# Attention stage: which engine copies the turned probabilities, in which order, and what is loaded first

## The reference, cut to what matters

```
q, k = rms_norm(q, q_gain), rms_norm(k, k_gain)      # per head, 64 channels
q, k = rotate own tokens by their angles (cos, sin)  # x*cos + quarter_turn(x)*sin
for each block of 128 queries:
    own block:     keys = own tokens at distance <= 128, and all context tokens
    context block: keys = all context tokens
    s = q @ k.T * 64**-0.5        (masked outside the window)
    p = softmax over keys and one extra "sink" logit per head (the sink's share is dropped)
    o = p @ v
```

## Time and profile before

| | us |
|---|---|
| median of 3 runs (5364.80 to 5377.84) | 5374.77 |
| the profiled execution | 5348.35 |
| its span in the trace | 5346.5 |
| attention stage, 3246.3 to 3589.7 from the span's start | 343 |

### The profile page before, as it was taken

The page is one execution under the profiler, slowest core; times in us unless marked ns, Lnnn a source line. Parts: engine busy times, 40 slices in busy tenths (PEclk is TensorE's granted clock), DMA queues, the critical chain, the costliest instruction groups (busy, mean ns, idle before and its releaser), DMA issues. The chain is left out here.

```text
span 5346.5 us, 88289 instructions
## 1 busy us (share of the span) xinstructions
PE 4436.9 (83%) x38298; PEld 3427.1 (64%) x38298; DVE 2537.0 (47%) x3635; ACT 1577.8 (30%) x2467; POOL 509.3 (10%) x483
## 2 busy tenths in 40 slices
PE   5999968888887687865878866768999899687999
PEld 4888757777776455652222344447888788576787
DVE  4556666667664674532000033554444322476553
ACT  3222223333322453421000032433222212563322
POOL 0000011100110465000000001330000000000000
PEclk8999979999998799987999977889999999898999
DMA  6656710000001110423999531112112133212232
GB/s 227 236 197 218 265 46 14 14 14 14 14 6 36 36 50 30 173 92 120 422 422 422 232 124 52 33 52 73 64 64 69 62 110 127 76 46 84 85 102 92
DMA packets 169889, 616.55 MB, mean 115 GB/s; under 512 B 24176, under 2 KB 37489, under 8 KB 144177
## 3 DMA queue, kind: packets, MB, share of 16 engines
q1 hardware_dynamic: 156224, 551.37, 28.4%
q0 software_dynamic: 13296, 59.77, 2.8%
HBM read 533.32 MB, written 77.75 MB: 114 GB/s over the span
## 5 line engine op out<-in xcount | busy, mean ns | idle before, releaser
L1885 PE MATMUL f_acc<-f_a_lo,f_w_hi 128*128 128x512 f32 x4048 | 1027.3, 356 | 65.6 <-DVE f_a_lo L2107 31.6
L1885 PEld LDWEIGHTS f_acc<-f_a_lo,f_w_hi 128*128 128x128 f32 x4048 | 666.4, 190 | 189.4 <-issue 43.5
L1885 PE MATMUL f_acc<-f_a_lo,f_w_lo 128*128 128x512 f32 x2288 | 687.9, 356 | 0.0
L1874 DVE TENSOR_TENSOR f_w_lo<-f_w_raw,f_w_hi 128x1024 fp32r<-128x1024 f32 (+1 forms) x176 | 228.4, 1298 | 527.5 <-ACT f_w_hi L1869 527.5
L1885 PEld LDWEIGHTS f_acc<-f_a_lo,f_w_lo 128*128 128x128 f32 x2288 | 377.1, 189 | 62.4
L1869 ACT CAST f_w_hi<-f_w_raw 128x1024 fp32r<-128x1024 f32 (+1 forms) x176 | 194.5, 1105 | 593.5 <-DMA f_w_raw<-in_ffn_w_up 209.9
L1885 PE MATMUL i_acc<-i_x_hi,i_w_hi 128*128 128x512 f32 (+1 forms) x1024 | 306.1, 354 | 12.2 <-DVE i_x_lo L2640 11.9
L335 DVE COPY_PREDICATED rw_work<-rw_mask_x,rw_big 128x512 f32<-128x512 uint8 x288 | 238.7, 881 | 154.5 <-PE rw_big L626 149.3
L1885 PE MATMUL i_acc<-i_x_lo,i_w_hi 128*128 128x512 f32 (+1 forms) x1024 | 304.9, 353 | 0.0
L1885 PE MATMUL i_acc<-i_x_hi,i_w_lo 128*128 128x512 f32 (+1 forms) x1024 | 304.7, 353 | 0.0
L1389 PE MATMUL ex_big<-ex_w,ex_xe_now 128*64 128x512 f32 x1024 | 237.6, 619 | 76.5 <-DMA ex_w<-in_exp_w 76.5
(11 more groups left out here) (521 smaller groups left out, 8036.4 us busy)
## 6 DMA issues: line engine op xcount, KB each, us to landing
ex_w<-in_exp_w SPq DMA_DIRECT2D x192, 1024.0 KB, 17.5
i_mod_rows<-in_ada_rows SPq DMA_DIRECT2D x128, 512.0 KB, 4.9
f_w_raw<-in_ffn_w_up SPq DMA_DIRECT2D x88, 512.0 KB, 3.3
i_w_raw<-in_w_in_both SPq DMA_DIRECT2D x44, 512.0 KB, 3.7
f_w_raw<-in_ffn_w_down SPq DMA_DIRECT2D x32, 704.0 KB, 4.1
i_w_raw<-in_w_in_lat SPq DMA_DIRECT2D x40, 512.0 KB, 4.8
pt<-i_stage POOLq DMA_DIRECT2D x22, 768.0 KB, 6.3
f_w_raw<-in_hgrn_w_both SPq DMA_DIRECT2D x24, 512.0 KB, 3.2
```

The costliest lines, as they stand in the source:

```text
L1874: dve.tensor_tensor(self.view(self.w_lo, u), self.view(self.w_raw, u), self.view(self.w_hi, u).bitcast(F32), ALU.subtract).then_inc(self.r ...
L1885: op = pe.matmul(acc[:, a:b], part[:, k], xs[:, k0 + k, a:b], start=(first and k == 0 and part is w_hi and xs is x_hi), stop=(last and k = ...
```

## The change

It makes three edits, all in `attention`.

1. The second group of turned tiles (k = 1), which the pairs with 512 and 640 columns have, is copied by ACT and not by DVE. The copy stands first in ACT's step, ahead of `exponentials(s+2)` or `logs(s+2)`. It has a semaphore of its own, so PE waits for two semaphores where it waited for one; `copies_until` counts both. 32 of 48 pairs have such a copy.
2. On DVE `copy_turned(s, 0)` stands ahead of `denominators(s+1)`.
3. `load(0)` is issued ahead of the constants. These are on two semaphores: four that the sums need (`first_in`) and four others (`const_in`). PE starts its loop after `first_in`; ACT starts after the small memset of DVE; the scores and the cosines wait for `consts_done` themselves.

```diff
+        def copies_until(n, k):
+            act_share = sum(1 for m in range(n) if len(turns(m % BLOCKS)) > 1) + (k > 1)
+            return turned_until[n] + k - act_share, act_share
...
-                for dst, src in ((ident, "ident"), (blockones, "blockones"), (turn, "turn"), (cos, "cos"), (sin, "sin"), (mask, "window")):
-                    sp.dma_start(dst[:], consts[src]).then_inc(S["const_in"], 16)
-                sp.dma_start(sink[:], sinks).then_inc(S["const_in"], 16)
-                sp.dma_start(gain[:], gains).then_inc(S["const_in"], 16)
...
                 load(0)
+                for dst, src in ((blockones[:], consts["blockones"]), (ident[:], consts["ident"]), (gain[:], gains), (turn[:], consts["turn"])):
+                    sp.dma_start(dst, src).then_inc(S["first_in"], 16)
+                for dst, src in ((cos[:], consts["cos"]), (sin[:], consts["sin"]), (mask[:], consts["window"]), (sink[:], sinks)):
+                    sp.dma_start(dst, src).then_inc(S["const_in"], 16)
                 load(1)
...
                 def consts_prepared():
-                    dve.memset(eps[:], 1e-6)
-                    dve.wait_ge(S["const_in"], 128)
+                    dve.wait_ge(S["first_in"], 64)
+                    dve.wait_ge(S["const_in"], 64)
...
                 def copy_turned(s, k):
+                    if k == 1:
+                        return
...
+                dve.memset(eps[:], 1e-6).then_inc(S["eps_done"], 1)
                 consts_prepared()
                 for s in STEPS:
                     groups = len(turns(pair_of(s)[1])) if kind(s) == "pair" else 0
+                    if groups:
+                        copy_turned(s, 0)
                     if kind(s + 1) == "pair":
                         denominators(s + 1)
-                    if groups:
-                        copy_turned(s, 0)
...
+                def copy_turned(s):                      # on ACT
+                    n = index(s)
+                    tiles = turns(pair_of(s)[1])[1]
+                    act.wait_ge(S["pt_ready"], turned_until[n] + 2)
+                    act.copy(pt_s[:, n % 2, tiles[0] * CH:(tiles[-1] + 1) * CH], big[:, T_BANK, 0:len(tiles) * CH]).then_inc(S["pt_copied_act"], 1)
...
-                act.wait_ge(S["consts_done"], 1)
+                act.wait_ge(S["eps_done"], 1)
                 square(0)
                 for s in STEPS:
+                    if kind(s) == "pair" and len(turns(pair_of(s)[1])) > 1:
+                        copy_turned(s)
                     if kind(s + 2) == "pair":
                         exponentials(s + 2)
...
                 def cosines(g):                          # on POOL
                     pool.wait_ge(S["normed"], g + 1)
+                    pool.wait_ge(S["consts_done"], 1)
...
                     pe.wait_ge(S["roped"], g + 1)        # in scores
+                    pe.wait_ge(S["consts_done"], 1)
...
                     if turned_until[n] + k:              # in turned
-                        pe.wait_ge(S["pt_copied"], turned_until[n] + k)
+                        by_dve, by_act = copies_until(n, k)
+                        pe.wait_ge(S["pt_copied"], by_dve)
+                        if by_act:
+                            pe.wait_ge(S["pt_copied_act"], by_act)
...
                     if first:                            # in values
-                        pe.wait_ge(S["pt_copied"], turned_until[n + 1])
+                        by_dve, by_act = copies_until(n + 1, 0)
+                        pe.wait_ge(S["pt_copied"], by_dve)
+                        pe.wait_ge(S["pt_copied_act"], by_act)
...
-                pe.wait_ge(S["consts_done"], 1)
+                pe.wait_ge(S["first_in"], 64)
```

More of the change, by code:

```diff
@@ L1498, in attention @@
         S = {n: ctx.sem(f"at_{n}") for n in (
-            "const_in head_in0 head_in1 consts_done squares sums_ready rstd_logs rstd_done vt_copied normed turn_ready cos_done roped shared_done scores maxed exped den_done scaled "
-            "pt_ready pt_copied pv_ready o_copied stored0 stored1").split()}
+            "first_in const_in eps_done head_in0 head_in1 consts_done squares sums_ready rstd_logs rstd_done vt_copied normed turn_ready cos_done roped shared_done scores maxed exped den_done scaled "
+            "pt_ready pt_copied pt_copied_act pv_ready o_copied stored0 stored1").split()}
         def pair_of(s):
```

## The result

The changed kernel is faster: a ratio of 0.9941 to the kernel before, 95% interval 0.9919 to 0.9963 (medians 5347.93 us of 7 runs against 5369.99 of 7); timed again it was 0.9951, 0.9933 to 0.9969 (medians 5340.43 and 5369.2). One of the seven executions of the changed kernel was in a slower state of the chip (5635.42 us) and is left out of the ratio. The sign and the mechanism were right, the size was too small.

What follows compares the result with a forecast made beforehand. A ring of waits between ACT and DVE, with POOL's scaling holding up DVE, was taken as the bound. Terms 11.9 + 4.8 + 3.8 - 1 = 19.5 us off; from 5374.8 this gave 5355 us, range 5342 to 5368.

Steps and rivals of the forecast that it cites:

- the ring: Attention stage's cycle: exponentials on ACT, denominators then maxima on DVE, exponentials again, each engine idle while the other works.
- b1 to b2: Between exponentials' starts of a half's second and third blocks: stays 5.09 us, POOL's scaling time plus 0.32 setting the step.
- b0 to b1: Between exponentials' starts of a half's first two blocks: 4.46 us forecast against 4.73, POOL's scaling holding up DVE.
- Plain halves: Halves without sums or turn: 4 x 2.6 us plus 1.5 for the last, together 11.9 us gained.
- b3 to b4: Between exponentials' starts of a half's fourth and fifth blocks: 4.48 us forecast, against 5.67 at low clock.
- b5 to b0: From the exponentials of a half's last block to the next half's first: PE bounds it, about 4.0 us against 4.63.
- b4 to b5: Between exponentials' starts of a half's last two blocks: 3.86 us forecast against 5.06, or 4.4 to 4.9 in others.
- Sums and turn: The three halves holding sums and turn: 1.4 us in each of three groups, with the sums' 0.2 together 4.8 us.
- P2 to P3: Between two pairs' exponentials, across the sums and logarithms: 0.2 us gained for a group, between -1 and +1.
- Waits: PE's added waits before most transposes and values, some 140: 0.02 us each where PE is on path, -1 us.
- the copy on the ring: Rival: ACT's copies stand in front of waiting exponentials; 17 us slower, 5392; chance 0.03.
- The low clock: Rival: PE at low clock takes the ring's place in steps b3 to b0; gain only 11 us, 5364; chance 0.25.

Runs made afterwards that it cites:

- the second profile: The changed kernel profiled again with no edit; attention stage 318.8 us, ratio 0.9951 to the kernel before.

## Why the prediction was right and wrong

- *The copy is not on the ring in the wide steps; POOL's scaling is.* Right, to 0.02 us: b1 to b2 5.09 before and after, b0 to b1 4.45. Halving POOL's work (4.35), and using instructions that POOL does not hold up (4.70, with 0.35 us more of their own), showed the cause.
- *Plain halves, 11.9 us.* Measured 10.7, and 11.8 in the second profile. Right. Most single steps too: b3 to b4 4.48 forecast, 4.46 to 4.93 measured; b5 to b0 4.0 against 3.74 to 3.91; b4 to b5 3.86 against 3.97 to 5.05, too low. That the sum still came out is in part luck: the 0.5 us of a half that I took off for a low clock at b3 to b4 was lost mostly at b4 to b5.
- *Sums and turn, 4.8 us.* **This term was mis-sized**: 9.4 us, 8.0 in the second profile. At P2 to P3 I had 0.2 us net for a group and measured 1.0, 1.6 and 1.7. Behind P2's exponentials PE starts the sums 1.2, 0.4 and 1.2 us earlier, where I had 0.4 for each, and its eight passes took 2.75, 3.40 and 2.75 us after against 2.75, 4.86 and 3.37 before. The granted clock at the sums rose from 0.56 to 0.81 in the second group and from 0.81 to 1.00 in the third. I had nothing for it in the sum. The passes of the second group, before and after, with the columns of the earlier trace rows:

```profile
3379.59:3384.45 4.86, 4.86 (x11) 2.67 (x11) 1.02 (x3) 1.55 (x2) 2.46 (x2) 0.56 0.40 162
...
3385.51:3388.90 3.39, 3.39 (x11) 1.93 (x11) 0.93 (x3) 0.61 (x4) 2.04 (x2) 0.81 0.54 216
```

  The second profile repeats this (2.74, 3.28 and 2.75), and with the loads alone the second and third group are as before (4.87 and 3.37). Why the clock was granted so stays open: from P1's exponentials to these sums PE's longer idle gaps were 2.3 us after and 2.9 to 3.0 before, but with ACT's copy alone they were 2.6 and the passes took 4.24 and 4.21 us at 0.65. At the step P5 to P6 I had nearly the right amount (1.2 measured, 1.4 forecast), and none for P4 to P5, where 0.3 to 0.7 came.
- *First loads, 3.8 us.* Right: squares 3.8 us earlier (3.6 in the second profile); 3.4 to 4.4 at the first exponentials.
- *Waits, -1 us.* No row gave the 0.02 us for a wait, and no run measures it. None was seen: b5 to b0, where I had PE on the path, came out shorter than forecast.
- *ACT's copy costs nothing in a plain half.* Right, with little to spare: doubled, it costs 3 to 4 us in the three plain halves of the first three groups and nothing in the two of the last group; of the 11 to 12 us of the whole most lie at the sums.
- *The baseline.* My time was counted from a median of three runs (5374.8); with seven it was 5370.0. So the forecast time stood for a gain of 15 us and not of 19.5; the 5 us were noise of the starting point. The 13 us that I called the spread of medians of three were the spread of the three runs themselves. Of the 31.7 us of the first ratio, the stage's traces show 23.3; the rest is no more than its interval allows.
- *The new order costs 0.26 us in a step.* This held only for all parts together. The prediction never asked what the order does without ACT's copy, and my forecast for that run, 2 to 6 us shorter, was wrong in sign: it is the largest loss of all that was tried but one.
- Of the rivals, the copy on the ring did not come. The low clock did come in one of the shortened steps, b3 to b4, at 0.50 to 0.71 of full speed; in the last group, where it had been 0.97 to 1.00, it is 0.67 to 0.71 now. It did not halve the gain: b3 to b4 is still 4.46 to 4.93 (5.67 before in the first three groups), and b5 to b0 and b0 to b1 ran at full clock. The step in the second group, before and after:

```profile
3434.13:3439.80 5.67, 4.17 (x18) 2.52 (x20) 3.06 (x8) 1.54 (x5) 2.04 (x2) 0.50 0.00 0
...
3437.43:3442.36 4.93, 4.35 (x26) 2.85 (x26) 3.20 (x7) 2.12 (x7) 2.04 (x2) 0.65 0.00 0
```

## What to carry to other kernels

Before counting a removed instruction, look for a place in the same trace where the step already runs without it: rows 5 and 6 gave the new step times to 0.02 us. Parts of a change to a ring of waits don't add: an order that cost 12.5 us alone was worth 11 beside the edit that made its inputs early, so judge each part by undoing it from the whole as well. And where a tiny instruction takes five times its usual time, look at which engine works beside it: rewriting it brought b1 to b2 from 5.09 to 4.70 us, though the stage got shorter (by 7 to 8 us) only when one of the steps on DVE went as well.

## What was not expected of the hardware

A DVE instruction of 128x2 elements took 0.16 us alone and up to 1.17 us beside POOL's scaling, while a per-partition scalar form of it took 0.34 us for two and was never held up. The eight passes of the sums, the same code in every kernel here, took from 2.74 us at a granted clock of 1.00 to 5.16 us at 0.53 (in the run with the copy behind the exponentials). With the loads alone this made P2 to P3 of the first group 1.6 us longer, though nothing in that step was edited, and it blurs edits that are worth less than this.
